# Delta rule loop: the four copies that bring the turned later rows together, two on VectorE and two on ScalarE

## The reference, cut to what matters

```python
def chunk_gated_delta(q, k, v, g, beta, s0):
    ...
    gamma = jnp.exp(jnp.where(tri, gc[..., :, None] - gc[..., None, :], NEG_INF))
    kb = kc * bc[..., None]
    a_mat = jnp.where(strict, jnp.einsum('nbhid,nbhjd->nbhij', kb, kc) * gamma, 0.0) + jnp.eye(C_CHUNK, dtype=jnp.float32)
    rhs = jnp.concatenate([vc * bc[..., None], kb * jnp.exp(gc)[..., None]], axis=-1)
    sol = lax.linalg.triangular_solve(a_mat, rhs, left_side=True, lower=True)
    ...
    def step(S, xs):
        u_i, w_i, a_i, qd, kd, gl = xs
        v_new = u_i - jnp.einsum('bhck,bhkv->bhcv', w_i, S)
        o = jnp.einsum('bhck,bhkv->bhcv', qd, S) + jnp.einsum('bhij,bhjv->bhiv', a_i, v_new)
        S = S * jnp.exp(gl)[..., None, None] + jnp.einsum('bhck,bhcv->bhkv', kd, v_new)
        return S, o
```

## Time and profile before

| | us |
|---|---|
| median of 3 runs | 3975.45 |
| lowest and highest | 3971.19, 3984.16 |
| profiled execution | 3984.25 |
| its span in the profile | 3982.5 |

### The profile page before, as it was taken

The page is one execution under the profiler, slowest core; times in us unless marked ns, Lnnn a source line. Parts: engine busy times, 40 slices in busy tenths (PEclk is TensorE's granted clock), DMA queues, the critical chain, the costliest instruction groups (busy, mean ns, idle before and its releaser), DMA issues. The chain is left out here.

```text
span 3982.5 us, 60796 instructions
## 1 busy us (share of the span) xinstructions
PE 3452.1 (87%) x24657; PEld 2547.5 (64%) x24657; DVE 2260.6 (57%) x3458; ACT 1720.0 (43%) x2624; POOL 618.2 (16%) x508
## 2 busy tenths in 40 slices
PE   5979878898959999999699975887859599999995
PEld 1469845664746666666499964666747466666663
DVE  5153333243477878878531444444664778878884
ACT  2031155101336556656311133657843366655663
POOL 0020041211100001000120001407731000001100
PEclk9989989898979999999899987888989799999997
DMA  4133195512447888887453328017425478888775
GB/s 171 64 131 100 54 306 182 179 57 92 167 172 276 294 294 292 280 287 277 167 137 98 97 106 293 15 40 227 145 91 193 150 278 295 293 296 297 282 269 204
DMA packets 378635, 761.46 MB, mean 191 GB/s; under 512 B 88840, under 2 KB 218423, under 8 KB 377192
## 3 DMA queue, kind: packets, MB, share of 16 engines
q1 hardware_dynamic: 358090, 697.66, 49.5%
q0 software_dynamic: 17648, 59.50, 6.2%
q10 hardware_dynamic: 2618, 0.40, 0.1%
HBM read 643.02 MB, written 115.10 MB: 190 GB/s over the span
## 5 line engine op out<-in xcount | busy, mean ns | idle before, releaser
L2536 DVE TENSOR_TENSOR moe_w_low<-ffn_w,moe_w_high 128x1024 fp32r<-128x1024 f32 x768 | 897.3, 1220 | 91.5 <-ACT moe_w_high L2461 89.1
L2461 ACT ACTIVATE moe_w_high<-ffn_w 128x1024 fp32r<-128x1024 f32 x768 | 777.8, 1053 | 192.9 <-DMA ffn_w<-moe_w_gate 126.9
L2387 PE MATMUL moe_small<-ffn_w,ffn_xpT 128*16 128x512 f32 x2048 | 238.3, 594 | 0.0
L2365 PE MATMUL moe_G<-moe_w_high,moe_xT_high 128*128 128x512 f32 x512 | 185.3, 443 | 16.4 <-DVE moe_xT_low L2499 9.6
L224 PE MATMUL proj_mm<-proj_hT_low,proj_w_high 128*128 128x384 f32 x576 | 193.2, 335 | 0.0
L224 PE MATMUL proj_mm<-proj_hT_high,proj_w_low 128*128 128x384 f32 x576 | 193.1, 335 | 0.0
L224 PE MATMUL proj_mm<-proj_hT_high,proj_w_high 128*128 128x384 f32 x576 | 193.1, 335 | 0.0
L224 PE MATMUL proj_mm<-proj_w_high,proj_hT_high 128*128 128x416 f32 (+1 forms) x504 | 178.0, 353 | 12.3 <-POOL proj_hT_low L344 8.5
L2313 POOL DMA_INDIRECT scratch_x<-moe_ys,keep_slot_s x32 | 50.6, 1581 | 866.6 <-DVE moe_ys L2528 866.6
L224 PE MATMUL proj_mm<-proj_w_high,proj_hT_low 128*128 128x416 f32 (+1 forms) x504 | 176.8, 351 | 0.0
L224 PE MATMUL proj_mm<-proj_w_low,proj_hT_high 128*128 128x416 f32 (+1 forms) x504 | 175.6, 348 | 0.0
(11 more groups left out here) (496 smaller groups left out, 7123.4 us busy)
## 6 DMA issues: line engine op xcount, KB each, us to landing
ffn_w<-moe_w_gate SPq DMA_DIRECT2D x256, 512.0 KB, 6.1
ffn_w<-moe_w_up SPq DMA_DIRECT2D x256, 512.0 KB, 6.9
ffn_w<-moe_w_down SPq DMA_DIRECT2D x256, 512.0 KB, 5.3
attnrun_m_w<-w_ada SPq DMA_DIRECT2D x40, 1024.0 KB, 11.2
scratch_conv<-proj_zf POOLq DMA_DIRECT2D x24, 512.0 KB, 2.9
scratch_tm<-proj_tm SPq DMA_DIRECT2D x45, 208.0 KB, 2.0
scratch_spec<-front_room SPq DMA_DIRECT2D x36, 256.0 KB, 2.1
proj_w_raw<-even_w_in SPq DMA_DIRECT2D x24, 384.0 KB, 4.1
```

Source lines behind the costliest of these rows:

```text
L2365: mm = nc.tensor.matmul(bank[:, half, :], stat[a][:, k, :], cut[b][:, half * BANK:(half + 1) * BANK], start=k == 0 and i == 0, stop=k == K ...
L2387: nc.tensor.matmul(out, stat, w, start=k == 0, stop=k == KD - 1, tile_position=(0, 32 * q)).then_inc(small_done, 1)
L2461: nc.scalar.activation(w_high[n % CUT_ROOM][:], raw_rows(wall, n), ACT.Copy).then_inc(w_up, 1)
L2536: nc.vector.tensor_tensor(w_low[n % CUT_ROOM][:], raw_rows(wall, n), w_high[n % CUT_ROOM][:].bitcast(F32), ALU.subtract).then_inc(w_cut, 1)
```

## The change

A new semaphore `TB_taken` counts VectorE's copies, two an item. `TT_taken` now counts four an item: two copies of `take_later`, which does the even heads only (`bb[0]`), and two of `take_all`. VectorE does the odd heads' copies (`bb[1]`), behind `r` and ahead of `take_w(n, 1)`, and waits there until the odd heads are turned. TensorE waits for both counts ahead of `level_u(n, 1)` and ahead of `turn(n, 2)`.

```diff
+        TB_taken = s.sem("TB_taken")
...
         def taken(n, li, r):
 
-            return 6 * n + (2 * r + 2 if li < LAST else 5 + r)
+            return 4 * n + (2 if li < LAST else 3 + r)
+
+        def later_rows(n, r):
+            d = items[n][1]
+            return [(slice(32 * (2 * x + 1 - d), 32 * (2 * x + 1 - d) + 32), slice(HALF * r + 32 * x, HALF * r + 32 * x + 32)) for x in range(2)]
...
             def turn(n, li):
                 pe.wait_ge(U_done, u_count(n, li - 1))
                 if n or li == LAST:
-                    pe.wait_ge(TT_taken, 6 * n if li < LAST else taken(n, 1, 1))
+                    pe.wait_ge(TT_taken, 4 * n if li < LAST else taken(n, 1, 1))
+                if li == LAST:
+                    pe.wait_ge(TB_taken, 2 * n + 2)
...
                 else:
                     pe.wait_ge(TT_taken, taken(n, li, 1))
+                if li == 1:
+                    pe.wait_ge(TB_taken, 2 * n + 2)
...
             def take_later(n):
-                d = items[n][1]
-                for r in range(2):
-                    act.wait_ge(T_turned, turned(n, 1, r))
-                    for x in range(2):
-                        src = slice(32 * (2 * x + 1 - d), 32 * (2 * x + 1 - d) + 32)
-                        dst = slice(HALF * r + 32 * x, HALF * r + 32 * x + 32)
-                        nc.scalar.activation(TT1[dst], bb[r][src], ACT.Copy).then_inc(TT_taken, 1)
+                act.wait_ge(T_turned, turned(n, 1, 0))
+                for src, dst in later_rows(n, 0):
+                    nc.scalar.activation(TT1[dst], bb[0][src], ACT.Copy).then_inc(TT_taken, 1)
...
                 if live:
+                    dve.wait_ge(T_turned, turned(n, 1, 1))
+                    for src, dst in later_rows(n, 1):
+                        nc.vector.tensor_copy(TT1[dst], bb[1][src]).then_inc(TB_taken, 1)
                     take_w(n, 1)
```

## The result

The changed kernel is slower: 4046.91 us (median of 6 runs, 4037.29 to 4052.24) against 3980.05 us for the kernel before (6 runs, 3971.19 to 3987.59). The ratio is 1.0167, with an interval of 1.0149 to 1.0185. The forecast was 3988.9 us with a range up to 3998, so the cost (66.9 us) is about five times the 13.4 us predicted. The profiled execution took 4037.29 us, its span is 4035.1.

What follows compares the result with a forecast made beforehand. In `delta_chunks`, ScalarE's copies release `level_u(n, 1)` and VectorE's row of work releases `turn(n, 2)`. VectorE's row +10.6 and the clock +2.8 gave +13.4 us on 3975.45, so 3988.9 us, range 3979 to 3998.

Steps and rivals of the forecast that it cites:

- What leaves ScalarE: ScalarE in `delta_chunks`: two of four copies go, 1.2 us an item; exponential and `kg` come earlier, worth nothing by itself.
- With GpSimd 1.2 us earlier and S 1.07 us later the two don't meet: Items 13 and 16: scaling of `S` no longer stalls beside GpSimd's addition into `o`; these items change by only -0.06 us.
- What comes onto VectorE: Two PSUM copies between L3348 and L3306: 0.68 to 0.69 us each, 0.73 us from start to start.
- r + 4.14: Start of the level 1 subtraction on VectorE, counted from r, the start of L3348; before, r + 3.38 in item 9.
- `level_u(n, 1)` keeps its 0.62 us, now for VectorE's `W`: TensorE ahead of `level_u(n, 1)`: the 0.62 us wait stays, its releaser changing from ScalarE's copies to VectorE.
- Sum of the row of work: VectorE's delay of the level 1 subtraction: 13 items x 0.80, item 7 0.3, items 13 and 16 -0.1; together +10.6 us.
- The clock: TensorE's longer rests in the loop make its clock fall in two more items, +2.8 us.
- every second item with 9.8 us: Rival: TensorE's clock falls in every second of 14 items; +20.4 us in total, 3996 us, chance 0.12.
- TensorE's own stalls take it up: Rival: rests elsewhere shorten TensorE's "issue" stalls, or copies follow at 0.61, halving the cost; +5, 3980 us, chance 0.15.
- Item of 12.7 us: Sign in the profile after: one item of the loop takes 12.7 us, where it took about 11.9.

Runs made afterwards that it cites:

- e1: Changed kernel plus two further ScalarE copies into a tile nobody reads, so the exponential and `kg` come as late as before: 3995.73 us, ratio 1.0034.
- e4: Changed kernel with the scaling of `S` moved behind the level 1 subtraction on VectorE, `kg` staying early: 3977.17 us, ratio 0.9983 against the kernel before.
- e6: Kernel before, with only the scaling of `S` moved behind the level 1 subtraction: 3996.66 us, ratio 1.0031.
- e5: Kernel before, with the exponential ahead of ScalarE's four copies and no copy on VectorE: 4002.01 us, ratio 1.0048.

## Why the prediction was wrong

- **What leaves ScalarE. The step that failed.** The prediction had `kg` come 1.2 us earlier and the scaling of `S` 1.07 us later, and wrote of the first "That is worth nothing by itself", since TensorE doesn't wait for `kg`. It asked who waits for GpSimd, not whom GpSimd holds. The rows needed were in the trace of before: VectorE's `S` in item 9 ended at 2828.25, and GpSimd's next instruction was

```profile
2829.40 2.37 POOL L3388 TENSOR_TENSOR gdnc_kg<-gdnc_kg,gdnc_gam 128x1024 f32<-128x1024 f32 x1 [1.88 <-ACT gdnc_gam L3260]
```

  The gap between them was 1.15 us. The change moves one by 1.2 and the other by 1.1, towards each other, 2.3 in all. The size was to be had too: `kg` 2.37 and `TA` 1.07 instead of two free instructions of 0.43. Even the sign of a hold was there. `S` took 1.03 us in this item, not the 0.86 of item 5, and its first instruction lay beside the end of another GpSimd instruction, which ran to 2827.52:

```profile
2826.48 1.04 POOL L3412 TENSOR_TENSOR gdnc_kd<-gdnc_kv,gdnc_egk 128x512 f32<-128x512 f32 x1
```

- **"With GpSimd 1.2 us earlier and S 1.07 us later the two don't meet".** True of the addition into `o` (L3416), the one GpSimd instruction that I looked at the earlier trace rows, and in item 13 the hold came nevertheless, from `kg`. The Trainium skill (SBUF — State Buffer, section "SBUF: two separate sides") was quoted in that very place: a VectorE instruction with two SBUF inputs and a GpSimd one that reads SBUF exclude each other for their whole length. The trace after agrees (3.77 instead of 0.86 beside `kg`); I used the rule to explain away one stall and didn't ask it of GpSimd's other instructions.
- **What comes onto VectorE. Right.** The two copies take 1.40 to 1.42 us with 0.72 from one start to the next (forecast 0.69 and 0.73). They are never held: of the 36, none took over 698 ns, though in the later items they lie beside GpSimd's addition into `o` for 1.1 us (in item 13 from 2949.57, the addition from 2949.02 for 1.66 us). In e1 the subtraction starts at r + 4.11 (2829.72 - 2825.61; forecast r + 4.14), `turn(n, 2)` waits 0.97 (forecast 1.05). In the kernel after it is r + 7.02.
- **`level_u(n, 1)` keeps its 0.62 us, now for VectorE's `W`. Right** (0.62 in the item above). ScalarE's rest ahead of its copies is 3.20 us instead of 1.59; how much of that is the hold's, the rows don't separate.
- **Sum of the row of work, +10.6.** With the hold taken away (e1) the wait for the subtraction is 19.2 - 9.8 = 9.4 us longer. Right within 1.2 us.
- **The clock, +2.8.** Too small even without the hold: in e1 VectorE waits 46.1 - 38.3 = 7.8 us longer for `level_w(n, 2)`. In an item of e1 the turns took 1.83 us behind a rest of 0.97:

```profile
2816.33 1.83 PE L3133 MATMUL gdnc_b<-keep_ident,gdnc_T 128*128 128x128 f32 x8 [0.97 <-DVE gdnc_T L3325]
```

  while those of 2830.52 took 1.09 behind the same 0.97. Its rival, every second item with 9.8 us, was nearer.
- **TensorE's own stalls take it up.** This rival was right on its own: "issue" fell from 8.6 us to 1.9 in e1 and 0.8 after. In e1 it about offsets what the clock term lacked: 9.4 + 7.8 - 6.7 = 10.5, and 1.6 more for a longer wait ahead of `level_u(n, 1)` (10.6 and 3.0 instead of 11.4 and 0.6), 12.1 in all. The run gave 13 and the forecast had 13.4, so that even without the hold the sum would have come out right in part by two errors that cancel.
- **Item of 12.7 us.** After: about 17.1 us in the items with the hold (+5.2 over before: 2.9 hold, 0.8 copies, 1.5 clock), 14.2 from item 16 to 17. In e1, without the hold, five undisturbed items take 12.6 to 12.7, as forecast; the others take longer.

## What to carry to other kernels

When work leaves an engine, follow everything that comes earlier through it down to GpSimd, and when work is put on VectorE, everything that comes later; then lay the two engines side by side and look for VectorE instructions with two SBUF inputs that now lie beside a GpSimd instruction. An engine that nobody waits for can still hold another. Where such an instruction sits ahead of the one that TensorE waits for, move the load only as far as the gap between the two engines allows: here 1.15 us, enough for one copy (-7 us) and not for two (+67 us). Or look whether it can stand behind the urgent one instead (e4, -7 us with both copies), and check what is then behind it (e6, +12 us).

## What the runs showed that I had not expected

- A pair of VectorE instructions of 0.43 us each took up to 3.77 us (2.58 + 1.17) beside GpSimd instructions of 2.36 and 1.24 us. The second one didn't follow the first: GpSimd's next instruction came in between and held it again.
- Starting first saves a pair only its first instruction: in e5 `S` started 0.31 us ahead of `kg` and took 3.14 us. GpSimd's own instructions became longer by little (`TA` 1.24 instead of 1.07).
- The hold makes TensorE rest for 3.9 us an item, and the clock then falls in those items: 14 us of the 51 between e1 and the kernel after.
- Adding two useless ScalarE copies an item made the changed kernel 51 us faster.
